# One encoder step on one core: selection masks built beside attention units, and the results of two attention stages copied out by ScalarE

## The reference, cut to what matters

```
A: score[q,s] = sum_h relu(qi_h . ki_s) * wi_h      sel = top 256 keys (top 80 for the sample)
   out = softmax(q k^T / 8 over the selected keys) v
B: latent mixer: keys and values expanded from a 128-wide latent;  out = softmax(...) v
C: forgetting attention, softmax with a bias;  D: stick-breaking, no softmax:
   a[q,s] = sigmoid(z[q,s]) * prod over s < r < q of (1 - sigmoid(z[q,r]));   out = a v
```

## Time and profile before

| | |
|---|---|
| three runs, median (lowest to highest) | 3200.12 us (3197.18 to 3205.57) |
| the profiled execution, its own time | 3197.15 us |
| its span, first to last instruction | 3195.4 us |
| PE busy in the span | 2974.4 us (93%) |
| DVE, ACT busy | 1728.6 us (54%), 1277.4 us (40%) |
| stage b, start of the first and the last PE group | 290.92 and 509.88 us |
| stage a, likewise | 530.10 and 667.14 us |
| stage d, likewise | 2104.91 and 2268.27 us |

### The profile page before, as it was taken

How to read it: one execution, slowest core, us unless ns; L and a number is a source line. 1 busy time by engine, 2 the same in 40 slices (tenths; PEclk the granted TensorE clock), 3 DMA queues, 4 the chain that set the end, 5 groups by cost and what they waited for, 6 DMA issues and landing times. The chain is left out here.

```text
span 3195.4 us, 48791 instructions
## 1 busy us (share of the span) xinstructions
PE 2974.4 (93%) x17421; PEld 2524.2 (79%) x17421; DVE 1728.6 (54%) x3768; ACT 1277.4 (40%) x2682; POOL 168.4 (5%) x240
## 2 busy tenths in 40 slices
PE   8986885998999999999899799988889999999998
PEld 6752553677999999999799567855679999999998
DVE  5438998764444444544431664168654444445555
ACT  4436994543222222222243455367532222222223
POOL 0000222310000000000000330000000000000000
PEclk9986997999999999999999899999999999999999
DMA  4120001021111111111311201110201111111111
GB/s 145 54 49 1 13 14 47 1 77 56 40 39 53 39 39 53 39 39 53 124 55 50 80 2 64 56 57 1 77 27 40 39 52 40 39 48 43 39 42 74
DMA packets 146189, 151.96 MB, mean 48 GB/s; under 512 B 17116, under 2 KB 122196, under 8 KB 146068
## 3 DMA queue, kind: packets, MB, share of 16 engines
q1 hardware_dynamic: 146068, 150.44, 15.2%
HBM read 126.65 MB, written 23.24 MB: 47 GB/s over the span
## 5 line engine op out<-in xcount | busy, mean ns | idle before, releaser
L247 PE MATMUL ffn_up<-hlow_r,ffn_uhi 128*128 128x384 f32 (+1 forms) x2112 | 690.8, 327 | 0.0
L2177 DVE SCALAR_TENSOR_TENSOR ffn_cv<-ffn_G,ffn_ctap,ffn_cv 128x256 f32<-128x256 f32 (+1 forms) x352 | 168.8, 500 | 492.0 <-ACT ffn_cv L2103 487.4
L247 PEld LDWEIGHTS ffn_up<-hlow_r,ffn_uhi 128*128 128x128 f32 x2112 | 398.2, 189 | 0.9
L2097 ACT ACTIVATE ffn_G<-ffn_up 128x384 f32<-128x384 f32 (+2 forms) x176 | 65.2, 397 | 821.6 <-PE ffn_up L248 821.6
L2210 DVE TENSOR_TENSOR xres<-ffn_dn,xres 128x512 f32<-128x512 f32 (+1 forms) x396 | 263.6, 686 | 132.4 <-PE ffn_dn L248 121.1
L246 PE MATMUL ffn_dn<-ffn_dhi,ffn_ahi 128*128 128x512 f32 x704 | 280.6, 399 | 2.9
L248 PE MATMUL ffn_dn<-ffn_dhi,ffn_alo 128*128 128x512 f32 x704 | 278.4, 395 | 0.0
L247 PE MATMUL ffn_dn<-ffn_dlo_r,ffn_ahi 128*128 128x512 f32 x704 | 278.3, 395 | 0.0
L246 PE MATMUL ffn_up<-mixed_a_r,ffn_uhi 128*128 128x384 f32 (+1 forms) x528 | 174.7, 331 | 4.1 <-DVE ulo_r L2154 4.1
L246 PE MATMUL ffn_up<-mixed_c_r,ffn_uhi 128*128 128x384 f32 (+1 forms) x528 | 174.7, 331 | 4.1 <-DVE ulo_r L2154 4.1
L246 PE MATMUL ffn_up<-mixed_b_r,ffn_uhi 128*128 128x384 f32 (+1 forms) x528 | 174.1, 330 | 0.0
(11 more groups left out here) (473 smaller groups left out, 6927.1 us busy)
## 6 DMA issues: line engine op xcount, KB each, us to landing
ulo<-in_w_up_dram SPq DMA_DIRECT2D x44, 512.0 KB, 5.0
ffn_ulo<-in_w_up_dram SPq DMA_DIRECT2D x44, 512.0 KB, 4.7
ffn_dlo<-in_w_down_dram SPq DMA_DIRECT2D x22, 1024.0 KB, 4.9
w_d<-in_w_in_odd_dram SPq DMA_DIRECT2D x7, 768.0 KB, 9.6
proj_even_x<-in_x_prompt_dram SPq DMA_DIRECT2D x8, 512.0 KB, 3.3
xres<-in_x_prompt_dram SPq DMA_DIRECT2D x8, 512.0 KB, 4.4
scratch_x<-xres SPq DMA_DIRECT2D x8, 512.0 KB, 4.0
x_d<-scratch_x SPq DMA_DIRECT2D x8, 512.0 KB, 3.9
```

The costliest lines, as they stand in the source:

```text
L247: nc.tensor.matmul(out, lh, rl, start=False, stop=False)
L2097: s.activation(G[:, g0:g0 + w], upbank(c, b, 0)[:, j:j + w], ACT.Copy).then_inc(g_out, 1)
L2177: last = v.scalar_tensor_tensor(cv[:, 0, j:j + w], G[:, g0 - 2 + tapno:g0 - 2 + tapno + w], ctap[:, c, tapno:tapno + 1], cv[:, 0, j:j + w] ...
```

## The change

The six parts of it:

1. `search_steps`: one step in each of slots 0 to 29, two in slots 16 and 25. `next_float` goes to slot 30, `room_for_ties` to slot 31.
2. `select` is cut into five parts. The masks of tiles 2, 3, 4 and 5 are built in slots 32 to 35 of stage b (`CHOSEN_B`). Those of tiles 6 and 7 move to stage a, one part at the end of each of slots 0 to 9 (`CHOSEN_A`), and `peak` of a unit with t = 6 or 7 waits for them.
3. In stage a the list of units begins with tiles 0 to 5 of pairs 0 and 1, then tiles 6 and 7 of both.
4. The ten rounds for the sample move from slots 1 to 10 to slots 12 to 21 of stage a.
5. Stage a gets a scratch tile for the masks, and its `ahead` falls from 3 to 2.
6. In stages b and d `output` is done by ACT: that of unit i - 2 at the start of slot i. In d the load of the next activation table comes behind the last one.

```diff
--- before.py
+++ after.py
@@ -864,7 +864,8 @@
 
 PAIRS = 4
 ALL = [(p, t) for p in range(PAIRS) for t in range(TILES)]
-SAMPLE_LAST = [(p, t) for p in range(PAIRS) for t in range(NT)] + [(p, NT) for p in range(PAIRS)]
+SAMPLE_LAST = ([(p, t) for p in range(2) for t in range(6)] + [(p, t) for p in range(2) for t in (6, 7)] +
+               [(p, t) for p in range(2, PAIRS) for t in range(NT)] + [(p, NT) for p in range(PAIRS)])
 EXPAND = {1: [0, 1], 2: [2], 3: [3], 4: [4], 5: [5], 6: [6], 7: [7], 8: [8]}
 
 
@@ -893,21 +894,24 @@
 
 TPB = 3
 STEPS = 32
-TWICE, ONCE = (6, 7), (1, 2, 3, 4, 5)
+TWICE, SEARCH_ENDS = (16, 25), 29
 
 
 def search_steps():
 
     at, done = {}, 0
-    for i, (p, t) in enumerate(ALL):
-        n = min(STEPS - done, 2 if t in TWICE else 1 if t in ONCE else 0)
+    for i in range(len(ALL)):
+        n = (2 if i in TWICE else 1) if i <= SEARCH_ENDS else 0
         at[i] = list(range(done, done + n))
         done += n
+    assert done == STEPS
     return at
 
 
 SEARCH_AT = search_steps()
-SEARCH_ENDS = max(i for i in SEARCH_AT if SEARCH_AT[i])
+CHOSEN_B = {32: 2, 33: 3, 34: 4, 35: 5}
+CHOSEN_A = (6, 7)
+ROUNDS_FROM = 12
 
 
 class Groups:
@@ -970,14 +974,17 @@
             q, wkv, q_in, w_in = (soon[x] for x in ("q", "wkv", "q_in", "w_in"))
             k = [[sb(f"k{s}{h}", [96, KEYS]) for h in range(2)] for s in range(2)]
             v = [sb(f"v{s}", [P, KT, P]) for s in range(2)]
-            top, work, n_top = src["top"], src["work"], len(SEARCHED)
+            n_top = len(SEARCHED)
             wide = [0] + [sum(key_tile(t)[0] for t in SEARCHED[:j + 1]) for j in range(n_top)]
             below = sb("below", [P, wide[-1]], BF16)
-            tie, beyond = below[:, 0:SEQ], below[:, SEQ:2 * SEQ]
-            spare, up = sb("spare", [P, n_top]), sb("up", [P, n_top], mybir.dt.int32)
+            up = sb("up", [P, n_top], mybir.dt.int32)
             counted = {"dve": sem("counted_dve"), "act": sem("counted_act")}
-            settled, cand_ready, told = sem("settled"), sem("cand_ready"), sem("told")
-        ahead = 2 if fox else 3
+            settled, cand_ready = sem("settled"), sem("cand_ready")
+        if mla or dsa:
+            top, work, spare, told = src["top"], src["work"], src["top"]["spare"], sem("told")
+            scratch = below if mla else sb("scratch", [P, 2 * SEQ], BF16)
+            tie, beyond = scratch[:, 0:SEQ], scratch[:, SEQ:2 * SEQ]
+        ahead = 3 if stick or mla else 2
         ring = ahead + 1
         prob = [[sb(f"prob{s}{h}", [P, SEQ]) for h in range(2)] for s in range(ring)]
         if mla or fox:
@@ -1246,6 +1253,12 @@
                         act.wait_ge(tp_ready, FROM + groups.transposed(i - ring))
                     s_.activation(prob[i % ring][h][0:n, c0:c0 + cw], scores_of(i, h, n, c), ACT.Sigmoid).then_inc(taken_done[h], 1)
 
+            def output(i):
+                p, t = order[i]
+                n = queries(t)
+                act.wait_ge(pv_done, FROM + i + 1)
+                s_.activation(home[:, p, t * P:t * P + n], O[:, 0:n], ACT.Copy).then_inc(o_out, 1)
+
             def exponential(i, h):
                 p, t = order[i]
                 n, s, w = queries(t), i % ring, key_tile(t)[0]
@@ -1269,10 +1282,14 @@
                     for c in range(len(chunks(i))):
                         sigmoids(i, c)
                 for i in range(n_units):
+                    if i >= 2:
+                        output(i - 2)
                     for c in range(2):
                         pieces_of(act, "act", i, "t", c)
                         if i + ahead < n_units and c < len(chunks(i + ahead)):
                             sigmoids(i + ahead, c)
+                for i in (n_units - 2, n_units - 1):
+                    output(i)
                 s_.preload_act_table_set("sqrt_and_others")
                 return
             if mla:
@@ -1282,6 +1299,8 @@
             for i, h in ((0, 0), (0, 1), (1, 0), (1, 1))[:ahead + 1]:
                 exponential(i, h)
             for i in range(n_units):
+                if mla and i >= 2:
+                    output(i - 2)
                 first, second = ((i + 2, 0), (i + 2, 1)) if ahead == 3 else ((i + 1, 1), (i + 2, 0))
                 pieces_of(act, "act", i, "t", 0)
                 if first[0] < n_units:
@@ -1295,6 +1314,9 @@
                     pieces_of(act, "act", i, "x")
                 if mla and SEARCH_AT[i]:
                     count_below(SEARCH_AT[i][-1])
+            if mla:
+                for i in (n_units - 2, n_units - 1):
+                    output(i)
             if not mla:
                 s_.preload_act_table_set("sqrt_and_others")
 
@@ -1308,6 +1330,8 @@
                 if i == 0 and not dsa:
                     dve.wait_ge(cleared, FROM + 2)
                 dve.wait_ge(s_ready[h], FROM + chunks_until(i))
+                if dsa and t in CHOSEN_A:
+                    dve.wait_ge(told, FROM + 5 * CHOSEN_A.index(t) + 5)
                 if dsa and t == NT:
                     dve.wait_ge(found, FROM + 2 * rounds + 1)
                 c = slice(2 * s + h, 2 * s + h + 1)
@@ -1415,23 +1439,28 @@
                 v_.tensor_scalar(spare[:], spare[:], TIE, None, ALU.mult).then_inc(told, 1)
                 dve.wait_ge(told, FROM + 8)
 
-            def select(j):
-
-                t = SEARCHED[j]
-                w, n = work[t][:], key_tile(t)[0]
+            def select(t, told_before, part):
+
+
+                j, n = SEARCHED.index(t), key_tile(t)[0]
+                w = work[t][:]
                 out = src["bias"][:, src["bias_at"][t]:src["bias_at"][t] + n]
                 bar = top["bits"][:, j:j + 1].bitcast(F32)
                 tied, left_over = tie[:, 0:n], beyond[:, 0:n]
-                if j:
-                    dve.wait_ge(told, FROM + 8 + 5 * j)
-                v_.tensor_scalar(tied, w, bar, -TIE, ALU.is_equal, ALU.mult).then_inc(told, 1)
-                v_.tensor_scalar(out, w, bar, -TIE, ALU.is_lt, ALU.mult).then_inc(told, 1)
-                dve.wait_ge(told, FROM + 8 + 5 * j + 1)
-                v_.tensor_tensor_scan(left_over, tied, tied, spare[:, j:j + 1], ALU.add, ALU.bypass).then_inc(told, 1)
-                dve.wait_ge(told, FROM + 8 + 5 * j + 3)
-                v_.scalar_tensor_tensor(left_over, left_over, 0.0, tied, ALU.is_lt, ALU.mult).then_inc(told, 1)
-                dve.wait_ge(told, FROM + 8 + 5 * j + 4)
-                v_.tensor_tensor(out, left_over, out, ALU.add).then_inc(told, 1)
+                if part == 0:
+                    dve.wait_ge(told, FROM + told_before)
+                    v_.tensor_scalar(tied, w, bar, -TIE, ALU.is_equal, ALU.mult).then_inc(told, 1)
+                elif part == 1:
+                    v_.tensor_scalar(out, w, bar, -TIE, ALU.is_lt, ALU.mult).then_inc(told, 1)
+                elif part == 2:
+                    dve.wait_ge(told, FROM + told_before + 1)
+                    v_.tensor_tensor_scan(left_over, tied, tied, spare[:, j:j + 1], ALU.add, ALU.bypass).then_inc(told, 1)
+                elif part == 3:
+                    dve.wait_ge(told, FROM + told_before + 3)
+                    v_.scalar_tensor_tensor(left_over, left_over, 0.0, tied, ALU.is_lt, ALU.mult).then_inc(told, 1)
+                else:
+                    dve.wait_ge(told, FROM + told_before + 4)
+                    v_.tensor_tensor(out, left_over, out, ALU.add).then_inc(told, 1)
 
             if stick:
                 def remain(i):
@@ -1442,13 +1471,8 @@
 
                 for i in range(ahead - 1):
                     remain(i)
-                for i in range(n_units):
-                    if i >= 2:
-                        output(i - 2)
-                    if i + ahead - 1 < n_units:
-                        remain(i + ahead - 1)
-                for i in (n_units - 2, n_units - 1):
-                    output(i)
+                for i in range(n_units - ahead + 1):
+                    remain(i + ahead - 1)
                 return
             if mla:
                 for x in range(2):
@@ -1461,8 +1485,8 @@
                 over_sum(0, h)
             over_sum(1, 0)
             for i in range(n_units):
-                if dsa and 0 < i <= rounds:
-                    best_scores(i - 1)
+                if dsa and ROUNDS_FROM <= i < ROUNDS_FROM + rounds:
+                    best_scores(i - ROUNDS_FROM)
                 for c in range(2):
                     pieces_of(dve, "dve", i, "t", c)
                 if i + 1 < n_units:
@@ -1476,10 +1500,11 @@
                     settle(SEARCH_AT[i][0])
                 if i:
                     pieces_of(dve, "dve", i, "x")
-                    output(i - 1)
-                if dsa and 0 < i <= rounds:
-                    without_best(i - 1)
-                if dsa and i == rounds + 1:
+                    if not mla:
+                        output(i - 1)
+                if dsa and ROUNDS_FROM <= i < ROUNDS_FROM + rounds:
+                    without_best(i - ROUNDS_FROM)
```

(15 more changed lines are left out.)

3 lines of the change are left out of this document (2 added, 1 removed).

## The result

The changed kernel takes 3159.64 us in the median (3159.45 to 3160.09), the one before, beside it on the same chip, 3199.05 (3197.18 to 3205.57): ratio 0.9873, 95% interval 0.9856 to 0.9891, faster by 39.4 us. I had forecast 24 us (3176, range 3162 to 3190). Profile against profile it is 37.1 us (spans 3195.4 and 3158.3). The other 2.3 us come from which executions were profiled: that of the kernel before, 3197.15, lies 1.9 us under the median beside it, that of the changed kernel, 3160.09, 0.45 us over its own.

A forecast was written before the change was run, and what follows sets the result against it. Bounds: DVE and ACT in stage b's slots 0 to 26, DVE alone after; PE in stage a; in stage d DVE busiest, waiting for PE at copies. -20 + 5 - 9.3 = -24.3 from 3200.12 gives 3176 us, range 3162 to 3190.

The forecast's parts named there:

- stage b, slots 0 to 26: First part of stage b: two more search steps and 25 copies on ACT make it 159 us, +2.5.
- stage b, from slot 27 on: End of stage b, DVE alone: fewer steps, masks and copies there, 45.9 us for 68.4, -22.5.
- stage a: Stage a as a whole: masks sticking out by 3 us and less look-ahead +2, together +5, ends 0 and +19.
- stage d, with the table load: Stage d without copies in DVE's queue, the table load costing +1.3: 9.3 us faster, ends 4 and 16.
- I take 4 us left: Stage b, slots 0 to 26: idle time assumed left beside ACT's 154.9 us of work, giving 159.
- ACT's copies in stage b: Stage b: each result copy moved from DVE to ACT priced at 0.2 us, 25 in slots 0 to 26, eleven after.
- The second cost in stage a is that it looks only two units ahead ... +2: Stage a: look-ahead of two units adds 2 us, ends 0 and 8.5, as stage c's DVE waits for exponentials.
- 4 meetings in 10: Stage a: each of ten mask parts meets busy POOL 4 times in 10; 2 us, inside the masks' 3.
- stage a gives back more: Rival for stage a: masks paid in full and depth felt as in stage c, +19, 3190; half is 3183; chance 0.14.
- 2.3 us at each of the three changes of pair: Stage d: saved copies and earlier transposes, less ACT's added copies, make each change of pair 2.3 us shorter, 6.9 together.
- The end of the stage, for which I had 2.8 and 0.6: End of stage d: 2.8 us from the gap before the last transposes, 0.6 from the copies before it.
- more comes free: Rival: stage b -24, stage d -14, stage a +2, so -36, 3164, from DVE's 21.4 us of waits; chance 0.12.

The follow-up runs named there:

- b_out: The kernel before with only stage b's results copied by ACT, two units behind, search steps as before: 3198.13 us, ratio 0.9992.
- a_two: The kernel before with stage a looking two units ahead instead of three and nothing else: 3197.26 us, ratio 0.9988.
- masks_b: The changed kernel with the masks of tiles 6 and 7 built behind the last unit of stage b: 3167.83 us, ratio 0.9897.
- d_banks3: The kernel before, stage d's results alternating between two PSUM banks, one transpose bank given up, DVE copying unit i - 3: 3201.99 us, ratio 1.0002.
- d_late: The kernel before with DVE's copy of stage d's result moved behind the two scans of its slot: 3207.58 us, ratio 1.0018.
- b_dve: The changed kernel with stage b's results copied by DVE again: 3168.39 us, ratio 0.9896.

## Why the prediction missed

Forecast and measured, in us, from profile to profile:

| term | forecast | measured |
|---|---|---|
| stage b, slots 0 to 26 | +2.5 | -1.7 |
| stage b, from slot 27 on | -22.5 | -21.1 |
| stage a | +5 | +0.2 |
| stage d, with the table load | -9.3 | -13.5 |
| the rest | 0 | -1.0 |
| sum | -24.3 | -37.1 |

Three terms failed by 4 to 5 us each, all to the same side. The mechanisms of b and d were right and their sizes were not; in stage a the sign of one step was wrong.

- **Slots 0 to 26 of stage b.** ACT became the fuller engine, as said, with 152.6 us for the 154.9 forecast. The step that failed is "I take 4 us left": 1.4 were left. From the first scores to the end of slot 26 it is 161.5 us before and 159.8 now; both profiles have the early start.
- **Stage b from slot 27 on.** From 461.4 to stage a's first scores was 68.7 us, from 459.98 it is 47.6. DVE's work end to end, as said.
- **ACT's copies in stage b.** I gave them 0.2 us each on DVE. Beside the old steps they are worth 1.9 us, close to that price for the eleven behind slot 26 (b_out). Beside the new ones they are worth 9.2 to 9.7 in a profile that was slower than usual. 3.4 of it went when two idle times were filled. Some 5 would be DVE's 25 copies in a stretch where it has no idle time to put them, but no run shows that alone, and this stays open.
- **Stage a.** Two terms missed in opposite directions. "The second cost in stage a is that it looks only two units ahead ... +2" is wrong in sign: -3.8 (a_two). I had read stage c's waits as a cost of depth and had not looked at the ramp. The masks cost 4.0 to 4.8 for my 3 (masks_b), through POOL, which I had weighed at 4 meetings in 10 and which were all. The rival "stage a gives back more" named that mechanism; its price was hidden by the depth. That the sum came out near nothing is luck. -3.8 and +4.8 make +1.0, and the 0.8 to the +0.2 is within what the same code differs by.
- **Stage d.** The mechanism, the result copied out of DVE's queue, is right; "2.3 us at each of the three changes of pair" is mis-sized, they gave 2.9, 4.2 and 2.8. The end of the stage, for which I had 2.8 and 0.6, gave 5.5, and the first ramp took 0.5 instead of giving 0.3. Together that is 14.9 for the forecast's 10.6; the table load cost what I said, 1.3 us, and from the first scores to the output projection's first product it is 13.5 for 9.3 (167.35 us before, 153.82 now). I had counted the copies' work and one late start of transposes. What was missing is the wait for the copy itself, in front of the products of t = 5: 3.19 us at 2138.94, 3.19 at 2178.13, 1.63 at 2218.34 and 3.69 at 2257.53, 11.7 of PE's 14.6 us. Behind the second and the last of them PE also ran at half clock. I had read one change of pair of three, and it was the one with the short wait. The earlier trace rows had the clock: 2.83 us for 24 products, for which the earlier trace rows give 1.53. I used those rows for the stage's end only.
- **The rival "more comes free"** (3164) was nearest, but for a wrong reason: it counted DVE's 21.4 us of waits. In d_banks3 they fell to 7.4 us and stage d by 0.6; in d_late they fell to 14.5 and the stage grew by 7.2. PE's 14.6 us were what cost.

## What to carry to other kernels

Where two engines wait for each other through one buffer, look at both sides' waits and ask which side is on the path: the one that feeds the next stage of the pipe, not the one with the larger sum. A small copy belongs on the engine that is free when the buffer is full, or the buffer wants a second place; moving the copy within a busy queue only moves the wait. Size an event that repeats on all its occurrences, not on one: of the four waits in stage d, the one by which I sized the changes of pair was half as long as the others. And price a depth of look-ahead by its ramp as well as by its waits.

## What the runs showed of the hardware

- A short idle time can be followed by a loss of the clock that costs more than the idle time. Behind 1.14, 0.25 and 0.26 us idle in b_dve PE worked at the lower of its two levels, 1.2 for 2.4 GHz (4.60 us for scores that take 2.40, granted clock 0.50); where transposes filled the first of them it kept the upper one.
- The idle time alone does not decide it. Behind 1.30, 0.25 and 0.26 us idle, b_dve kept the clock (2.40 us at 470.90). Behind 3.19 us of waiting in stage d of the kernel before, 24 products took 1.53 us at 2138.94 and 2.83 at 2178.13. Behind the same 1.30 us at the start of stage b, the same code took 1.96 us in one execution and 3.56 in another.
- POOL is held up by DVE's mask instructions: POOL's mean for a 128 x 640 tile in stage a is 1120 ns in the changed kernel and 798 ns in masks_b, and two tiles of 512 keys took 3.46 us beside a scan of 2.33, without it 0.69 each.
- An ACT copy of 128 x 128 numbers out of PSUM costs ACT 0.16 us from start to start (354.56 to 354.72), though its row is 0.34 long.
